# Sample's FFN down projection as seven block products over pairs of f tiles, and the order of the four rows of tiles in sample's last norm

## The reference, cut to what matters

```python
h = _rmsnorm(x, norm_ffn_g)
u = jnp.einsum('bsd,df->bsf', h, w_up)                       # 1024 -> 2 x 2816
up = jnp.pad(u, ((0, 0), (1, 1), (0, 0)))
u = up[:, :-2] * conv_w[0] + up[:, 1:-1] * conv_w[1] + up[:, 2:] * conv_w[2] + conv_b
a, b = jnp.split(u, 2, axis=-1)
x = x + jnp.einsum('bsf,fd->bsd', jax.nn.silu(a) * b, w_down)  # 2816 -> 1024
...
return _rmsnorm(x, final_norm_g)
```

## Time and profile before

| | us |
|---|---|
| median of 3 runs | 2393.9 |
| lowest and highest | 2391.09, 2394.6 |
| the profiled execution | 2391.54 |
| its span | 2389.6 |
| PE busy in the span | 2329.2 (97%) |
| DVE, ACT, POOL busy | 1798.9, 1092.8, 1288.7 |
| first up matmul of sample | at 1374.7 |
| first product of prompt (after sample's group 21) | at about 1729.0 |

### The profile page before, as it was taken

One profiled execution on the slowest core, in us unless ns is written; L12 is line 12 of the kernel. 1 busy time (PEld: TensorE's weight loads), 2 busy tenths in 40 slices (PEclk: granted clock), 3 DMA queues, 4 the chain that ended last, 5 costly groups with the idle time before them and its releaser, 6 DMA issues.

```text
span 2389.6 us, 34203 instructions
## 1 busy us (share of the span) xinstructions
PE 2329.2 (97%) x12186; PEld 1993.3 (83%) x12186; DVE 1798.9 (75%) x2627; ACT 1092.8 (46%) x2147; POOL 1288.7 (54%) x1497
## 2 busy tenths in 40 slices
PE   7999999999999989999999999999989999999998
PEld 6998898888998968888878888888868888888886
DVE  7537777788889967566653379987768888888888
ACT  4426665656678852122332233433244444444444
POOL 5444635588877712043151055555556666666663
PEclk9999999999999999999999999999999999999999
DMA  8744434432222049888873342232253333332332
GB/s 296 250 172 149 159 131 159 154 143 104 79 79 85 13 151 313 305 285 296 281 259 132 106 150 97 89 106 97 84 202 94 97 93 102 93 102 93 100 95 110
DMA packets 153415, 352.69 MB, mean 148 GB/s; under 512 B 15776, under 2 KB 50976, under 8 KB 142752
## 3 DMA queue, kind: packets, MB, share of 16 engines
q1 hardware_dynamic: 151952, 350.12, 43.0%
q10 hardware_dynamic: 1296, 0.39, 0.1%
HBM read 268.67 MB, written 81.79 MB: 147 GB/s over the span
## 4 chain that ended last, share of the span: by engine, by line
PE 57%; DVE 3%; DMA 1%; POOL 1%; issue 1%; SPq 1%; ACT 0%; DVEq 0%; POOLq 0%; ACTq 0%
PE r_bank L2183 29%; PE r_bank L2060 10%; PE r_bank L2089 9%; PE r_bank L2122 5%; PE r_bank L2141 1%; PE r_bank L2170 1%; PE r_bank L2104 1%; DMA r_wxq_raw<-in_w_xq_heads 0%; DVE r_conv L2617 0%; DVE r_block L2610 0%; DVE r_prob L2598 0%; PE r_bank L2153 0%; DVE r_x_p L2833 0%; DVE r_x_p L2850 0%; POOL r_wxq_lo L1900 0%
## 5 line engine op out<-in xcount | busy, mean ns | idle before, releaser
L843 PE MATMUL t_proj<-t_w_hi,t_hbuf 128*128 128x384 f32 x1056 | 311.7, 348 | 2.1 <-ACT t_nat L994 0.7
L2705 DVE TENSOR_TENSOR r_x_p<-r_bank,r_x_p 128x512 f32<-128x512 f32 x280 | 183.0, 683 | 47.9 <-PE r_bank L2183 46.8
L1153 DVE TENSOR_REDUCE t_max_neg<-t_scores 128x1 f32<-128x1024 f32 (+1 forms) x192 | 197.0, 1038 | 23.8 <-PE t_scores L877 17.9
L1017 ACT ACTIVATE t_prob<-t_scores,t_max_neg 128x1024 f32<-128x1024 f32 (+1 forms) x192 | 187.4, 978 | 49.7 <-DVE t_max_neg L1153 45.5
L843 PEld LDWEIGHTS t_proj<-t_w_hi,t_hbuf 128*128 128x128 f32 x1056 | 194.9, 189 | 8.3 <-issue 6.8
L1026 ACT CAST t_pt_hi<-t_turn 128x512 fp32r<-128x512 f32 x240 | 140.3, 587 | 107.5 <-PE t_turn L896 82.3
L1173 DVE TENSOR_TENSOR t_pt_lo<-t_turn,t_pt_hi 128x512 fp32r<-128x512 f32 x240 | 163.5, 686 | 29.9 <-ACT t_pt_hi L1026 26.1
L843 PE MATMUL t_proj<-t_w_lo,t_hbuf 128*128 128x384 f32 x528 | 177.9, 337 | 0.0
L2617 DVE SCALAR_TENSOR_TENSOR r_conv<-r_rows,r_taps,r_conv 128x511 f32<-128x511 f32 (+3 forms) x134 | 157.0, 1172 | 27.0 <-ACT r_conv L2415 24.6
L1933 POOL TENSOR_TENSOR r_w_lo<-r_stage,r_w_hi 128x1024 fp32r<-128x1024 f32 x42 | 100.9, 2403 | 129.3 <-ACT r_w_hi L2354 129.3
L1949 POOL TENSOR_TENSOR r_s_lo<-r_s_raw,r_s_hi 128x512 fp32r<-128x512 f32 x87 | 131.7, 1519 | 63.2 <-ACT r_s_hi L2359 63.2
(11 more groups left out here) (318 smaller groups left out, 7315.2 us busy)
## 6 DMA issues: line engine op xcount, KB each, us to landing
t_hbuf<-split_x SPq DMA_DIRECT2D x60, 1024.0 KB, 4.8
block_sums<-r_block SPq DMA_DIRECT2D x128, 256.0 KB, 3.7
r_block<-in_w_up_units SPq DMA_DIRECT2D x88, 256.0 KB, 5.1
r_stage<-in_w_up_units SPq DMA_DIRECT2D x44, 512.0 KB, 3.3
r_s_raw<-block_sums SPq DMA_DIRECT2D x87, 256.0 KB, 2.7
r_w_raw<-in_w_up_units SPq DMA_DIRECT2D x66, 256.0 KB, 2.6
split_x<-t_hbuf SPq DMA_DIRECT2D x12, 1024.0 KB, 5.3
r_stage<-in_w_down SPq DMA_DIRECT2D x22, 512.0 KB, 3.3
```

The source lines that it names most:

```text
L843: ins = nc.tensor.matmul(proj_bank(i), l, r[:, k, :], start=(k == 0 and j == 0), stop=(k == KT - 1 and j == 2))
L1017: nc.scalar.activation(prob[:, n % PSLOTS, 0:p.keys], ps_s[:, n % 2, 0:p.keys], ACT.Exp, bias=max_neg[:, n % COLS:n % COLS + 1], accum_out ...
L1153: nc.vector.tensor_reduce(max_neg[:, n % COLS:n % COLS + 1], ps_s[:, n % 2, 0:p.keys], AX.X, ALU.max, negate=True).then_inc(max_done, 1)
L2705: nc.vector.tensor_tensor(x_p[:, t, cols], down_bank(q), x_p[:, t, cols], ALU.add).then_inc(p_add, 1)
```

## The change

The down projection of sample's f tiles 0 to 19 is done in ten pairs m of tiles (2m, 2m + 1). With the tokens cut into two halves of 256 and the columns into two of 512, each pair is a 2x2 block product by the same seven-product scheme as prompt's. A product is two token tiles of three matmuls: 42 matmuls a pair instead of 48. The tiles 20 and 21 stay as they were. Reduced to the core:

```diff
+S_ORDER = ("p7", "p1", "p4", "p6", "p5", "p2", "p3")
+S_WEAVE = ({(0, 5): "p7", (1, 1): "p1", (1, 4): "p4", (1, 7): "p6"}, {(0, 3): "p5", (1, 1): "p2", (1, 4): "p3"})
+S_LAST = {1: "p5", 3: "p2", 5: "p3"}
 # PE
+            def sample_pair(m, p):
+                n, w, left = s_weight(m, p), s_weight(m, p) % 3, LEFT[p]
+                before = n - {"p5": 1, "p2": 3}.get(p, 2)
+                pe.wait_ge(wd_ready, n + 1)
+                pe.wait_ge(a_ready, n + 1)
...
+                for q in range(2):
+                    if before >= 0:
+                        pe.wait_ge(s_add, 2 * before + q + 1)
+                    tile, place = slice(q * P, (q + 1) * P), one_bank((4 if p in ("p7", "p4", "p2") else 6) + q)
+                    three(place, b_hi[left][:, tile], b_lo[left][:, tile], sd_hi[w][:, :], sd_lo[w][:, :], p in OPENS, True,
+                          p not in OPENS).then_inc(s_down, 1)
             for i in range(1, FT):
+                weave = S_WEAVE[i % 2] if i > 1 else {}
                 for k in range(KT):
                     sample_up(i, 0, k)
+                    if i == LAST and k in S_LAST:
+                        sample_pair(PAIRS - 1, S_LAST[k])
+                    elif i < LAST and (0, k) in weave:
+                        sample_pair(i // 2 - 1, weave[0, k])
                 for k in range(KT):
                     sample_up(i, 1, k)
-                    for n in SAMPLE_WEAVE.get(k, ()):
-                        sample_down(i - 1, n)
+                    if i == LAST:
+                        for n in SAMPLE_WEAVE.get(k, ()):
+                            sample_down(FT - 2, n)
+                    elif (1, k) in weave:
+                        sample_pair(i // 2 - 1, weave[1, k])
 # POOL
-            split_down(0, 0)
-            split_down(0, 1)
             up_low(1, 0)
             up_low(1, 1)
             for i in range(1, FT):
-                if i < LAST:
+                m, even, more = i // 2 - 1, i % 2 == 0, i < LAST
+                if even:
+                    s_low(m, "p4")
+                    for name in ("s1", "s2", "s4"):
+                        b_sums(m, name)
+                else:
+                    if i > 1:
+                        s_low(m, "p2")
+                        s_low(m, "p3")
+                    if more:
+                        b_sums(m + 1, "s3")
+                if more:
                     up_low(i + 1, 0)
-                split_down(i, 0)
-                if i < LAST:
+                    for p in ("p6", "p5") if even else ("p7", "p1"):
+                        s_low(m if even else m + 1, p)
                     up_low(i + 1, 1)
                 else:
+                    s_low(FT - 2, 0)
+                    s_low(FT - 2, 1)
                     low(0, "w11")
                     low(0, "s1")
-                split_down(i, 1)
+                    s_low(FT - 1, 0)
+                    s_low(FT - 1, 1)
             low(0, "s2")
 # ACT
             for i in range(FT):
+                m, even, more = i // 2 - 1, i % 2 == 0, i < LAST
+                if even and i:
+                    s_high(m, "p4")
+                elif i > 1:
+                    s_high(m, "p2")
+                    s_high(m, "p3")
+                    b_high(m, "a12")
+                    b_high(m, "s4")
                 sample_mid(i, 0)
...
+                elif i:
+                    s_high(FT - 2, 0)
+                    s_high(FT - 2, 1)
                     high(0, "w11")
                     high(0, "s1")
                 sample_mid(i, 1)
-                if i == LAST:
+                if more:
+                    up_high(i + 1, 1)
+                else:
                     high(0, "s2")
...
+                if i >= FT - 2:
+                    act.wait_ge(s_prod, i + 1)
+                    act.wait_ge(s_down, S_REST + S_DOWNS if i == LAST else s_used(PAIRS - 1, "a11"))
+                    nc.scalar.copy(sg_hi[:, :], s_conv[:, 0, :]).then_inc(s_ghi, 1)
+            s_high(LAST, 0)
+            s_high(LAST, 1)
 # sample's last norm, ACT and DVE
-            sample_square(0)
-            sample_square(1)
+            sample_square(2)
+            sample_square(3)
...
-            sample_scale(0)
+            sample_scale(2)
...
-                if i == 1:
-                    dve.wait_ge(row_rstd, 2)
-                    sample_scale(2)
-                    sample_scale(3)
...
                 subtract_w22(i)
-                if i == LAST:
+                if i == 1:
+                    dve.wait_ge(row_rstd, 2)
+                    sample_scale(0)
+                    value_shifts(i)
+                    sample_scale(1)
+                    a_low(0, "s3")
+                elif i == LAST:
 # SP
                 n = down_at[m, p]
-                if n < 2:
-                    sp.wait_ge(y_sent, 16 * 2)
-                elif n == 2:
+                if n == S_WEIGHTS:
                     sp.wait_ge(up_done, 2 * LAST + 1)
+                elif n < S_WEIGHTS + 3:
+                    sp.wait_ge(y_sent, 16 * (n - S_WEIGHTS))
```

357 lines of the change are left out of this document (249 added, 108 removed).

## The result

| | before | after |
|---|---|---|
| median, lowest to highest (us) | 2394.25, 2391.09 to 2394.77 (4 runs) | 2411.72, 2410.13 to 2413.55 (4 runs) |
| ratio, 95% interval | | 1.0078, 1.0066 to 1.0090 |
| profiled execution, its span | 2391.54, 2389.6 | 2411.66, 2409.6 |

The change is slower by 17.5 us. I had forecast 2391.0, from 2382 to 2401.

A forecast was written before the change was run, and what follows sets the result against it. PE was taken as the bound, busy 97% of the span, with DVE next to supply waits. The terms -13.6 + 10 + 2.1 + 2.1 + 4.0 - 7.5 give -2.9 us: a median of 2391.0 us, range 2382 to 2401.

The forecast's parts named there:

- Fewer matmuls, -13.6: Sample's groups: ten pairs lose 6 matmuls each, 60 at 0.2267 us, -13.6 us; a pair falls to 31.28 us.
- DVE in iterations 2 to 11, +10: Five pairs with prompt steps: DVE, held by POOL, sets the pace at 33.5 to 34 us; +10 us, bounds 0 and 16.
- the usual air on top of the load: Upper bound for iterations 2 to 11: DVE's usual 1 us of air a pair stays on top, 16 us lost.
- DVE is the bound, slower: Rival, iterations 2 to 11: DVE is held more than walked, 35 to 38 us a pair, 2399 to 2414; chance 0.2.
- DVE keeps up: Rival, iterations 2 to 11: the holds fall away, term 0 to 4 instead of 10, 2381 to 2385; chance 0.32.
- at no cost: Group 1 has no downs any more and starts group 2 with weights ready; no time lost.
- Last group, +2.1 and +2.1: Sample's last group: p2's operands and tile 20's down weights come late, +2.1 us each, 1 to 3 each.
- Prompt's s2, +4.0: Prompt's first products: s2's low part waits in POOL's queue, so s2 starts 4.0 us later, 3 to 5.
- The clock at s2: Rival: PE's pause of about 4.4 us at s2 slows the clock, 2.8 us come back, 2394; chance 0.08.
- The norm, -7.5: Sample's last norm: pause -5.3, clock -2.8, scales and shifts +0.6; together -7.5 us, from -5 to -8.5.
- the sum is ready at 1772.4, when PE wants it: Sample's last norm: DVE's sum comes at about 1772.4, PE wants it at 1772.3, so the pause shrinks by 5.3 us.
- the scales stand behind the sum: Sample's last norm: DVE's two scales, 4.47 us, move behind the sum PE waits for, -4.5; before the next sum, +0.6.

The follow-up runs named there:

- e2: Changed kernel with GpSimd's low part of the up weights formed for only 64 of 1024 columns: 2390.41 us, 0.9992 of before.
- e10: Changed kernel with VectorE's prompt steps spread, sample's end reordered, row loads spread, p4's rounding later, and GpSimd's up-weight low part in two halves: 2378.46 us, 0.9932.
- e12: Changed kernel with VectorE's four prompt steps an iteration in iterations 2 to 12 in place of 1 to 11: 2408.98 us, 1.0060 of before.
- e4: Changed kernel with GpSimd's low part of prompt's s2 moved ahead of the two low parts of tile 21's down weights: 2405.37 us, 1.0051 of before.
- e3: Kernel before with only the norm's part of the change: 2392.57 us, 0.9996 of before.
- e8: The kernel of e3 with the loads of prompt's rows spread behind group 0's operand loads: 2389.28 us, 0.9982 of before.
- e11: The kernel of e8 with p4's high and low part made in prompt's group 2 and p7's load behind three operand loads: 2389.21 us, 0.9979 of before.
- e14: The kernel of e11 with the scales of tiles 0 and 1 right behind prompt's sum of s2, their stores earlier: 2386.21 us, 0.9965 of before.

## Why the prediction was wrong, point by point

In one line, forecast against measured spans: fewer matmuls -13.6 and -13.6; iterations 2 to 11 +10 and +17.0 (2.6 of it in group 12), with +5.3 for their start; the end of sample and s2 +8.2 and +10.5, and 2.3 more for the clock; the norm -7.5 and -1.3.

- **Fewer matmuls, -13.6: right.** Odd groups have 66 matmuls, and where nothing waits a pair takes 31.28 us (e2, e10).
- **DVE in iterations 2 to 11, +10: the mechanism was right, the size too small, and its start was missed.** The load was near: 33.7 us forecast, 34.0 to 34.1 measured. (The "24.9 unhindered" of the later pairs doesn't follow from the prediction's own 23.2; it changed no term.) The failed step is that this load "sets the pace at 33.5 to 34". The upper bound of that term, the usual air on top of the load, is what came: DVE also idles some 1.5 us a pair, of which this row shows 1.2, for ACT's high part of its own step, in the pair from 1501.54.

```profile
L2812 DVE TENSOR_TENSOR r_t_lo<-r_t_raw,r_t_hi 128x512 fp32r<-128x512 f32 x6 | 6.8, 1135 | 1.2 <-ACT r_t_hi L2539 1.2
```

  So 35.6 us a pair and 14.4 us in iterations 3 to 11. The rival "DVE is the bound, slower" had 35 to 38 us a pair and 2399 to 2414 in all; its numbers came true, but not its reason, as DVE was held little more than I had walked. It had 0.2, and "DVE keeps up" 0.32, although my own sum gave DVE 33.7 us of work in 31.28: against that, a possible shift of half a us in POOL was no ground for the higher chance.
- **Group 1 and the start of group 2 "at no cost": wrong, +5.3.** I had walked the even and odd group but not the entry, where four sums in a row stand ahead of the first two low parts. Each was held and took 2.5, 1.8, 1.8 and 2.8 us. PE's pause of 2.96 us and the lower clock behind it (some 2 us) are the loss. e12 and e2 took it away.
- **Last group, +2.1 and +2.1: right in place and size** (2.25 and 2.23 us). At w11, forecast 1.1 us late, PE waited 2.0; its load took 3.9 us, not 3.4.
- **Prompt's s2, +4.0: right in mechanism, too small.** With E for the end of sample's last group, the forecast was E + 8.2; measured E + 9.4, which is 5.4 later than before and outside my 3 to 5. The pause at s2 was 4.2 us where I had 4.4; the rest is w11's later start. (My own terms for w11 add up to E + 1.3, not 1.1.) e4 shows that the place in the queue was the whole cause of the pause at s2.
- **The clock at s2: the rival with 0.08 came true**, for 2.3 us: half clock stood behind the pause. My row against it showed a clock of 1.00 with PE busy for 1.67 of 4 us, not what follows one pause of 4 us; 0.08 was too sure. The four us behind the pause:

```profile
1752.30:1756.30 4.00, 4.00 (x10) 3.17 (x11) 0.00 (x0) 0.00 (x0) 4.00 (x4) 0.50 0.00 0
```

- **The norm, -7.5: wrong, -1.6 alone (e3).** The failed step is "the sum is ready at 1772.4, when PE wants it: -5.3 of the pause". The sum did come about then (1773.0 on the old scale), but PE also needed the low part of s4's weights, which I had left out: in e3 2.1 us of the pause stayed for it, and the clock behind it was 0.57, so the 2.8 us for the clock came back by little more than one. Two further steps were off. The load of w11 was issued 2.1 us sooner but took longer: 4.1 us in e3 and, with the row loads spread, 5.7 in e8, where ACT went on at 1767.17 for 1766.95 before; why it took longer no run here shows. And "the scales stand behind the sum" only moved them ahead of the next one: I priced that at +0.6, and it was a pause of 3.4 in e11 once the other waits were gone. e14 gets 5.9. In the changed kernel itself the stretch to group 3 is 1.0 us longer than before, with the 2.3 of half clock at s2 in it.

The signs I had named were good ones: I would have called the forecast wrong at over 3 us lost in a pair, and a pair lost 4.3 to 4.4.

## What to carry to other kernels

The period of an engine at its bound is more than its load: add the waits that it has already at a lower load (1.5 us on 34.1 here), and treat a load of 1.08 of the period as a verdict of slower, not as a term with a middle value. Where VectorE's steps read two SBUF operands beside a busy GpSimd, halve GpSimd's instructions and spread the steps before taking matmuls away: the same change was 0.8% slower without this and the mended queues, and 0.9% faster with them, of which 0.35% can be had without the change (e14). When a wait is to be taken away, look at every operand of the instruction that waits: the trace names only the one that came last. Walk the entry and the exit of a pipeline by themselves, and look at each queue there for what is due first.
